# A 1,024-token two-block network on one core: where the second feed-forward's combined inputs are formed

## The chip, the cores and the metric

One core of one Trainium2 chip. The metric is the device time of one execution in microseconds (us). All data is float32; TensorE (PE) multiplies it as pairs of rounded parts (below). The kernel is written by hand in five instruction queues: PE, ACT (ScalarE), DVE (VectorE), POOL (GpSimd) and SP, which issues the DMAs. Each queue runs in its written order, and semaphores are the only link between them.

## What is computed

The whole network is a first block (pooling mixer, attention, feed-forward, gated embedding) and a second one (modulation, a token mixer, a convolutional feed-forward). The change touches the second block's feed-forward alone:

```python
h = rms_norm_2(x, pre_ffn_g[l]) * (1.0 + sc2) + sh2      # x: 1024 tokens x 1024 channels
u = causal_dwconv(h @ w_up, conv_w, conv_b)              # w_up: 1024 x 5632, 3 taps
g, val = u[..., :2816], u[..., 2816:]
y = (jax.nn.gelu(g, approximate=True) * val) @ w_down    # w_down: 2816 x 1024
x = x + g2 * rms_norm_2(y, post_ffn_g[l])
```

## The kernel before, in words

**Numbers.** Channels lie on the 128 partitions, tokens along the row: `x_mid`, `y`, `h_hi` and `h_lo` hold 8 rows (k) of 128 channels by 1024 tokens; a half is 512 tokens. A value v is carried as a rounded high part (a cast by ACT) and a low part (v minus the high part, by DVE; for weights by POOL). A product is three matmuls: high x high, low input x high weight, high input x low weight.

**Tiles.** w_up has 44 column tiles of 128: gate tile i and up tile i, for i from 0 to 21. Tiles 0 and 1 are computed plainly, in PE's order gate 0 and up 0 (both interleaved, half 0 and then half 1), gate 1, up 1 (L1475 to L1497). From tile 2 (`PLAIN`) on, the gate and the up product of a pair are made together from seven half-sized products (`product`, L979) in the order UP_LOW, SUM_2, DIFF_3, SUM_1, UP_HIGH, GATE_HIGH, DIFF_4, a Strassen-like scheme. Four of them use combinations of the input's quarters: with lo and late the first and last four rows k, 0 and 1 the halves, DIFF_3 = late0 - lo0, SUM_2 = lo1 + DIFF_3, GATE_HIGH = late1 - SUM_2, SUM_1 = lo1 - lo0. The first three lie in `back_raw`, SUM_1 in `y`; each has a high part (`back_form_high`, ACT, L2416) and a low part (`back_form_low`, DVE, L3597). SUM_1's parts go over h_hi and h_lo. The weights' combinations are DVE's `weight_low_sum` and `weight_high_sum` (L2870, L2891); `fill_pair` on ACT (L1791) casts them and on POOL (L3854) makes the low parts, in slots that come free by products.

**Banks.** A bank is freed for SUM_1 when ACT has copied the sum of UP_LOW and SUM_2 (`back_part(i, "two", 1)`, L2477), which waits for DVE's `back_sum` (L3630), which waits for ACT's copy of UP_LOW (L2471). GATE_HIGH waits for the first gate read (`back_gate_read(i, 1)`, L3636). After every second pair comes a group of the down product (`down`, L1021): eight 128-channel outputs m, each 12 matmuls of 512 columns. From m = 2 on, it waits until output m - 2 has been taken from its bank: by ACT's copy into `y` in group 0 (L2464), by DVE's addition later (`back_add`, L3644). So `y` carries other data until group 0: the squares of the norm, the rows of the combinations.

**Forming h, and the combinations.** For each half, `normed_to_ffn` on DVE (L3535) writes x_mid * gain * norm of row k into one of two rows of `tmp` (L3550); ACT adds the shift and casts to h_hi (`h_row`, L2353), and DVE writes h_lo (`low`, L3538). Because `tmp` has two rows, row k waits for its own queue's h_lo. The shift itself is a column of `mod` for each k. The combinations need full values: POOL adds h_hi and h_lo back together (`rows_sum`, L4042: four instructions of two rows each for half 0, two for half 1's first rows), DVE does so for half 1's last rows (`late_rows`, L3607). POOL then forms DIFF_3 and SUM_2 (L4049, L4055), DVE SUM_1 and GATE_HIGH (L3615, L3622), two rows an instruction (q = 0, 1). `back_raw` lies over part of `x_mid`, so the forming waits until x_mid has been parked in memory by eight DMAs (L4385).

**Tile by tile.** A tile passes ACT's first tap (`tap_first`, L2391), two taps on DVE (`tap_rest`, L3567), ACT's gelu, DVE's product, and a high (ACT, `back_hidden_high`) and low part (DVE, `back_hidden_low`) for the down product. Plain tiles read their taps from the product's banks. Between the plain products and pair 2, DVE's order is (L3650 to L3668): last rows, taps and product of tile 0, its low part, SUM_1, taps (1, 0), weight sums, GATE_HIGH, low parts of SUM_2, DIFF_3, SUM_1, taps (1, 1), product of tile 1. ACT's is L2434 to L2453. A wait in any of these queues holds everything written behind it. At the end, pair 21 is followed by down groups 9 and 10, the additions of group 9 standing behind the product of tile 21 (L3697 to L3701).

```python
            for q in range(2):
                back_form_low(SUM_1, q)
            whole_rest(1, 1, pairs.whole(("up2", 1)))
            ffn_product(1)
```

## Time and profile before

| | us |
|---|---|
| median of 3 runs | 2787.8 (2786.1 to 2792.4) |
| the profiled execution | 2787.0 |
| its span | 2785.2 |
| PE busy | 2668.6 (96%) |
| DVE busy | 1634.5 (59%) |
| ACT busy | 1111.0 (40%) |
| POOL busy | 1079.3 (39%) |
| mean granted clock of PE | 0.987 of full |

The profiled execution is one run; its span is the time from its first to its last instruction, and 1.8 us lie around it. Busy shares say how much an engine worked over the whole span, not whether the others waited for it. All stretches below are in us from the span's start. The second feed-forward begins near 2061 us and its pair 2 near 2119 us.

### The profile page before, as it was taken

The page shows a single profiled execution, that of the slowest core. Times are in us where ns is not written, and L with a number is a line of the kernel's source. Part 1 is how long each engine was busy: PE and PEld are TensorE (multiplying, and loading weights), DVE is VectorE, ACT ScalarE, POOL GpSimd, SP SyncE. Part 2 cuts the span into 40 slices and gives each one's busy share as a digit, 9 for nine tenths or more (in the row PEclk, how much of TensorE's full clock was granted, in tenths as well). Part 3 has the DMA queues.
Part 4 walks back from the last instruction along what each step waited for, and adds up shares of the span by engine and source line. Part 5 has one row for each costly group of instructions (what it writes and reads, how often), then busy time and mean ns, then how long its engine had stood idle before and what let it go on. Part 6 is the DMA issues. An engine that isn't in the chain of part 4 may idle for free.

```text
span 2785.2 us, 31774 instructions
## 1 busy us (share of the span) xinstructions
PE 2668.6 (96%) x12096; PEld 2135.2 (77%) x12096; DVE 1634.5 (59%) x1877; ACT 1111.0 (40%) x1888; POOL 1079.3 (39%) x705
## 2 busy tenths in 40 slices
PE   8999989999999999999999999999987999999997
PEld 6666768888778888888877678778756888888885
DVE  6777776652855555555663646527367465565656
ACT  6666521113533333233353433455344433343343
POOL 2444422224444444344444321123445444444445
PEclk9999999999999999999999999999999999999999
DMA  3000034433111111111212111122321111111113
GB/s 120 23 24 24 3 122 154 153 118 114 38 46 61 46 61 61 46 46 61 70 44 101 62 39 38 43 70 72 121 83 32 59 46 46 61 46 61 60 46 136
DMA packets 72055, 185.03 MB, mean 66 GB/s; under 512 B 7384, under 2 KB 20952, under 8 KB 71776
## 3 DMA queue, kind: packets, MB, share of 16 engines
q1 hardware_dynamic: 71904, 183.01, 19.9%
q8 instruction: 96, 1.57, 0.2%
q14 instruction: 55, 0.45, 0.1%
HBM read 167.71 MB, written 15.27 MB: 66 GB/s over the span
## 4 chain that ended last, share of the span: by engine, by line
PE 81%; DVE 9%; issue 3%; ACT 3%; POOL 2%; DMA 1%; SPq 0%; DVEq 0%; POOLq 0%; ACTq 0%
PE psum_mem L998 27%; PE psum_mem L704 17%; PE psum_mem L1038 16%; PE psum_mem L766 2%; PE psum_mem L1190 2%; PE psum_mem L1195 2%; PE psum_mem L1192 2%; PE psum_mem L750 2%; PE psum_mem L801 1%; PE psum_mem L856 1%; PE psum_mem L804 1%; PE psum_mem L802 1%; PE psum_mem L1267 1%; POOL w_lo L3759 1%; PE psum_mem L1232 1%
## 5 line engine op out<-in xcount | busy, mean ns | idle before, releaser
L3851 POOL TENSOR_TENSOR w_lo<-w_raw,w_hi 128x512 fp32r<-128x512 f32 x298 | 434.1, 1463 | 498.1 <-ACT w_hi L1789 497.6
L3759 POOL TENSOR_TENSOR w_lo<-w_raw,w_hi 128x1024 fp32r<-128x1024 f32 (+2 forms) x105 | 236.1, 2249 | 636.5 <-ACT w_hi L1559 591.3
L1789 ACT CAST w_hi<-w_raw 128x512 fp32r<-128x512 f32 x298 | 182.5, 620 | 297.8 <-PE psum_mem L998 115.4
L998 PE MATMUL psum_mem<-h_hi,w_hi 128*128 128x512 f32 x672 | 265.0, 394 | 15.0 <-ACT norm_row L2426 8.5
L998 PE MATMUL psum_mem<-h_hi,w_lo 128*128 128x512 f32 x672 | 264.0, 393 | 0.6 <-POOL w_lo L3851 0.6
L998 PE MATMUL psum_mem<-h_lo,w_hi 128*128 128x512 f32 x672 | 263.8, 393 | 0.0
L704 PE MATMUL psum_mem<-h_hi,w_hi 128*128 128x512 f32 x736 | 234.8, 400 | 14.0 <-ACT h_hi L1593 8.8
L704 PE MATMUL psum_mem<-h_hi,w_lo 128*128 128x512 f32 x736 | 230.0, 394 | 3.5 <-POOL w_lo L3759 3.5
L704 PE MATMUL psum_mem<-h_lo,w_hi 128*128 128x512 f32 x736 | 230.7, 395 | 2.6 <-DVE h_lo L3483 2.2
L1559 ACT CAST w_hi<-w_raw 128x1024 fp32r<-128x1024 f32 (+2 forms) x105 | 100.2, 954 | 270.9 <-PE psum_mem L704 242.5
L704 PEld LDWEIGHTS psum_mem<-h_hi,w_hi 128*128 128x128 f32 x736 | 138.7, 191 | 47.3 <-ACT h_hi L1593 8.8
L704 PEld LDWEIGHTS psum_mem<-h_hi,w_lo 128*128 128x128 f32 x736 | 139.7, 190 | 35.1 <-POOL w_lo L3759 5.6
L704 PEld LDWEIGHTS psum_mem<-h_lo,w_hi 128*128 128x128 f32 x736 | 139.7, 190 | 34.6 <-DVE h_lo L3483 3.4
L2996 DVE TENSOR_TENSOR x_block<-x_block,psum_mem 128x1024 f32<-128x1024 f32 x88 | 107.3, 1219 | 93.8 <-PE psum_mem L1038 93.7
L998 PEld LDWEIGHTS psum_mem<-h_hi,w_hi 128*128 128x128 f32 x672 | 127.6, 190 | 44.3 <-ACT norm_row L2426 9.4
L998 PEld LDWEIGHTS psum_mem<-h_hi,w_lo 128*128 128x128 f32 x672 | 127.5, 190 | 27.9 <-POOL w_lo L3851 1.3
L998 PEld LDWEIGHTS psum_mem<-h_lo,w_hi 128*128 128x128 f32 x672 | 127.5, 190 | 26.8 <-DVE h_lo L2903 0.4
L3809 POOL TENSOR_TENSOR beta<-beta,left 128x128 f32<-128x128 f32 (+2 forms) x96 | 87.6, 914 | 142.5 <-DVE left L2702 141.6
L1190 PE MATMUL psum_mem<-h_hi,w_hi 128*128 128x512 f32 x272 | 113.2, 416 | 4.6 <-POOL state L3970 3.4
L3648 DVE TENSOR_TENSOR y_mem<-y_mem,psum_mem 128x1024 f32<-128x1024 f32 x72 | 87.5, 1216 | 48.1 <-PE psum_mem L1038 47.9
L1195 PE MATMUL psum_mem<-h_hi,w_lo 128*128 128x512 f32 x272 | 107.2, 394 | 0.0
L998 PE MATMUL psum_mem<-form_hi,w_hi 128*128 128x512 f32 x264 | 103.0, 390 | 3.8 <-ACT form_hi L1809 2.1
(457 smaller groups left out, 6333.2 us busy)
## 6 DMA issues: line engine op xcount, KB each, us to landing
w_raw<-in_w_up_b SPq DMA_DIRECT2D x44, 512.0 KB, 3.3
w_raw<-in_w_in_a SPq DMA_DIRECT2D x32, 512.0 KB, 3.4
ada_raw<-in_w_ada SPq DMA_DIRECT2D x64, 256.0 KB, 3.3
w_raw<-in_w_ffn_up SPq DMA_DIRECT2D x22, 512.0 KB, 3.2
w_raw<-in_w_ffn_gate SPq DMA_DIRECT2D x22, 512.0 KB, 3.3
w_raw<-in_w_ffn_down SPq DMA_DIRECT2D x22, 512.0 KB, 3.2
w_raw<-in_w_down_b SPq DMA_DIRECT2D x22, 512.0 KB, 3.3
merged<-in_w_ada SPq DMA_DIRECT2D x32, 256.0 KB, 3.2
```

Of the source, the lines that this page charges most:

```text
L704: made = e.matmul(pairs.half(use, half), wt, x[:, half_of(half)], start=at == 0 and part == 0, stop=at == len(rhs) - 1 and part == 2, skip ...
L998: made = e.matmul(out, wt, x, start=j <= DIFF_3 and k == 0 and part == 0, stop=k == KH - 1 and part == 2, skip_group_check=True)
L1038: made = e.matmul(out[:, half, :], wt, x[:, half_of(half)], start=i == 0 and part == 0, stop=i == FFN_GROUP - 1 and part == 2, skip_group_ ...
L1190: e.matmul(bank(6 + half), high, h_hi[:, k, cols], start=k == 0, stop=False, skip_group_check=True)
L1195: made = e.matmul(bank(6 + half), low, h_hi[:, k, cols], start=False, stop=k == KD - 1, skip_group_check=True)
L1559: e.copy(w_hi[:, i, 0:width], w_raw[:, i, 0:width]).then_inc(*S.of("w_hi", c))
L1789: e.copy(w_slot(w_hi, slot, of), source).then_inc(*S.of("w_hi", key))
L2996: e.tensor_tensor(x1[:, m, :], x1[:, m, :], down_banks(g, m), ALU.add).then_inc(*S.of("x1", (g, m)))
L3648: e.tensor_tensor(y[:, m, :], y[:, m, :], down_banks(g, m), ALU.add).then_inc(*S.of("y_add", (g, m)))
L3759: e.tensor_tensor(w_lo[:, i, 0:width], w_raw[:, i, 0:width], w_hi[:, i, 0:width].bitcast(F32), ALU.subtract).then_inc(*S.of("w_lo", c))
L3809: e.tensor_tensor(kept, kept, left[i % 3][:, HALF + 1 - width:HALF + 1], ALU.mult).then_inc(*S.of("weight", i))
L3851: e.tensor_tensor(w_slot(w_lo, slot, of), source, w_slot(w_hi, slot, of).bitcast(F32), ALU.subtract).then_inc(*S.of("w_lo", key))
```

## The change

Four things, in the order of the diff:

- The normalised rows (before the shift) are kept in `y` for all k, where they were in two rows of `tmp`; h_hi and h_lo are made from there. The wait of row k on the own h_lo is gone.
- The combinations are formed on DVE from these rows, the difference of shifts (`gain[:, 0:KH]`, 128x4) or the shift being added in the same instruction: DIFF_3, SUM_2 and GATE_HIGH by four instructions of one row each, SUM_1 by two of two rows as before. POOL's six sums and four combinations and DVE's two sums of last rows are gone.
- Orders. ACT: DIFF_3's high parts ahead of gelu of tile 0; tap (1, 0) behind SUM_2's; gelu of tile 1 behind all of pair 2's first fills; tile 1's high part behind two fills of down group 0. DVE: DIFF_3 and SUM_2 ahead of tile 0's taps; SUM_1 and GATE_HIGH behind its product; low parts in the order DIFF_3, SUM_2, then taps (1, 0), then SUM_1; taps (1, 1), product and low part of tile 1 behind pair 2's first gate read.
- At the end, the first two additions of down group 9 stand between the taps of tile 21 and its product; tile 21's low part follows the third.

```diff
@@ -2354,7 +2354,7 @@
                 cols = half_of(half)
                 w.wait_ge("normed", ("ffn2", k, half))
                 w.wait_ge("full", ("out2", KD - 1, 1))
-                e.activation(h_hi[:, k, cols], tmp[:, k % 2, cols], ACT.Identity,
+                e.activation(h_hi[:, k, cols], y[:, k, cols], ACT.Identity,
                              bias=mod[:, 3 * KD + k:3 * KD + k + 1], scale=1.0).then_inc(*S.of("h_hi", ("ffn2", k, half)))
 
...
@@ -2414,7 +2414,7 @@
             def back_form_high(j, q):
-                w.wait_ge("form_g" if j in (DIFF_3, SUM_2) else "form", ("b", j, q))
+                w.wait_ge("form", ("b", j, 2 * q + 1))
...
@@ -2434,14 +2434,13 @@
             plain_tap(0, 0)
             plain_tap(0, 1)
             unit()
-            gelu(0)
             for q in range(2):
                 back_form_high(DIFF_3, q)
+            gelu(0)
             back_hidden_high(0)
-            plain_tap(1, 0)
             for q in range(2):
                 back_form_high(SUM_2, q)
-            gelu(1)
+            plain_tap(1, 0)
             fill_pair(PLAIN, UP_LOW, "b")
             fill_pair(PLAIN, SUM_2, "b")
             for q in range(2):
@@ -2449,8 +2448,9 @@
             for q in range(2):
                 back_form_high(GATE_HIGH, q)
             fill_pair(PLAIN, DIFF_3, "b")
+            fill_pair(PLAIN, SUM_1, "b")
+            gelu(1)
             plain_tap(1, 1)
-            fill_pair(PLAIN, SUM_1, "b")
             taken[0], done[0] = len(units), len(units)
 
             for kind, at in FF_ORDER[PLAIN:-2]:
@@ -2475,7 +2475,8 @@
                 if i > PLAIN:
                     w.wait_ge("gate", ("b", i - 1, 0))
                 back_part(i, "two", 1)
-                back_hidden_high(i - 1)
+                if i > PLAIN:
+                    back_hidden_high(i - 1)
                 fill_pair(i, DIFF_4, "b")
                 w.wait_ge("full", ("gu2", i, SUM_1))
                 back_part(i, "four", 0)
@@ -2486,6 +2487,8 @@
                 else:
                     fill_pair(i + 1, UP_LOW, "b")
                     fill_pair(i + 1, SUM_2, "b")
+                if i == PLAIN:
+                    back_hidden_high(1)
                 w.wait_ge("gate", ("b", i, 0))
                 tap_first(i, 0, gate_in[:, :])
                 if g is None:
@@ -3537,7 +3540,7 @@
 
                 def low(k):
                     w.wait_ge("h_hi", ("ffn2", k, half))
-                    e.scalar_tensor_tensor(out=h_lo[:, k, cols], in0=tmp[:, k % 2, cols],
+                    e.scalar_tensor_tensor(out=h_lo[:, k, cols], in0=y[:, k, cols],
                                            scalar=mod[:, 3 * KD + k:3 * KD + k + 1],
                                            in1=h_hi[:, k, cols].bitcast(F32), op0=ALU.add,
                                            op1=ALU.subtract).then_inc(*S.of("h_lo", ("ffn2", k, half)))
@@ -3545,9 +3548,7 @@
                 w.own("x_mid")
                 w.wait_ge("x_mid_g", (MID_POOL[-1], half))
                 for k in range(KD):
-                    if k >= 2:
-                        w.own("h_lo")
-                    e.scalar_tensor_tensor(out=tmp[:, k % 2, cols], in0=x_mid[:, k, cols],
+                    e.scalar_tensor_tensor(out=y[:, k, cols], in0=x_mid[:, k, cols],
                                            scalar=gain[:, 2 * KD + k:2 * KD + k + 1], in1=norm, op0=ALU.mult,
                                            op1=ALU.mult).then_inc(*S.of("normed", ("ffn2", k, half)))
                     if k > 0:
@@ -3596,36 +3597,39 @@
 
             def back_form_low(j, q):
                 w.wait_ge("form_hi", ("b", j, q))
-                if j == DIFF_3:
-                    w.wait_ge("form_g", ("b", SUM_2, q))
                 low = back_form(back_lo_mem, h_lo, j, q)
                 source = y[:, two_rows(q), half_of(0)] if j == SUM_1 else back_form(back_raw, None, j, q)
...
-            def late_rows(q):
-                rows, cols = two_rows(q, 1), half_of(1)
-                w.wait_ge("sum", ("mid", 1))
-                w.wait_ge("h_hi", ("ffn2", KD - 1, 1))
-                w.own("h_lo")
-                e.tensor_tensor(y[:, rows, cols], h_hi[:, rows, cols].bitcast(F32), h_lo[:, rows, cols].bitcast(F32),
-                                ALU.add).then_inc(*S.of("form", ("b", "late", q)))
+            def shift(k):
+                return mod[:, 3 * KD + k:3 * KD + k + 1]
+
+            def back_form_three(k):
+                w.own("shift")
+                w.own("normed")
+                e.scalar_tensor_tensor(out=back_raw[:, BACK_FORMS.index(DIFF_3), k, :], in0=y[:, KH + k, half_of(0)],
+                                       scalar=gain[:, k:k + 1], in1=y[:, k, half_of(0)], op0=ALU.add,
+                                       op1=ALU.subtract).then_inc(*S.of("form", ("b", DIFF_3, k)))
+
+            def back_form_two(k):
+                w.own("form")
+                e.scalar_tensor_tensor(out=back_raw[:, BACK_FORMS.index(SUM_2), k, :], in0=y[:, k, half_of(1)],
+                                       scalar=shift(k), in1=back_raw[:, BACK_FORMS.index(DIFF_3), k, :], op0=ALU.add,
+                                       op1=ALU.add).then_inc(*S.of("form", ("b", SUM_2, k)))
+
+            def back_form_four(k):
+                w.own("form")
+                e.scalar_tensor_tensor(out=back_raw[:, BACK_FORMS.index(GATE_HIGH), k, :], in0=y[:, KH + k, half_of(1)],
+                                       scalar=shift(KH + k), in1=back_raw[:, BACK_FORMS.index(SUM_2), k, :],
+                                       op0=ALU.add, op1=ALU.subtract).then_inc(*S.of("form", ("b", GATE_HIGH, k)))
 
             def back_form_one(q):
                 rows = two_rows(q)
-                w.wait_ge("form_g", ("b", "rows", 1, q))
-                w.wait_ge("form_g", ("b", DIFF_3, q))
+                w.own("form")
                 e.tensor_tensor(y[:, rows, half_of(0)], y[:, rows, half_of(1)], y[:, rows, half_of(0)],
-                                ALU.subtract).then_inc(*S.of("form", ("b", SUM_1, q)))
-
-            def back_form_four(q):
-                w.own("form")
-                w.wait_ge("form_g", ("b", SUM_2, q))
-                e.tensor_tensor(back_form(back_raw, None, GATE_HIGH, q),
-                                y[:, two_rows(q, 1), half_of(1)],
-                                back_form(back_raw, None, SUM_2, q),
-                                ALU.subtract).then_inc(*S.of("form", ("b", GATE_HIGH, q)))
+                                ALU.subtract).then_inc(*S.of("form", ("b", SUM_1, 2 * q + 1)))
 
             def back_sum(i):
                 w.wait_ge("part", ("b", i, "low"))
@@ -3647,25 +3651,29 @@
-            for q in range(2):
-                late_rows(q)
+            for k in range(KD):
+                w.wait_ge(f"parked{k}", "mid")
+            e.tensor_tensor(gain[:, 0:KH], mod[:, 3 * KD + KH:4 * KD], mod[:, 3 * KD:3 * KD + KH],
+                            ALU.subtract).then_inc(*S.of("shift", 0))
+            for k in range(KH):
+                back_form_three(k)
+            for k in range(KH):
+                back_form_two(k)
             whole_rest(0, 0, pairs.whole(("gate2", 0)))
             whole_rest(0, 1, pairs.whole(("up2", 0)))
             ffn_product(0)
-            back_hidden_low(0)
             for q in range(2):
                 back_form_one(q)
-            whole_rest(1, 0, pairs.whole(("gate2", 1)))
+            for k in range(KH):
+                back_form_four(k)
+            back_hidden_low(0)
             weight_low_sum(PLAIN, "b")
-            for q in range(2):
-                back_form_four(q)
-            for j in (SUM_2, DIFF_3):
+            for j in (DIFF_3, SUM_2):
                 for q in range(2):
                     back_form_low(j, q)
+            whole_rest(1, 0, pairs.whole(("gate2", 1)))
             for q in range(2):
                 back_form_low(SUM_1, q)
-            whole_rest(1, 1, pairs.whole(("up2", 1)))
-            ffn_product(1)
 
             for kind, at in FF_ORDER[PLAIN:-2]:
                 if kind == "down":
@@ -3677,14 +3685,19 @@
                         if m == 3:
                             weight_low_sum(2 * at + 3, "b")
                     continue
-                i, g = at, down_behind(at)
+                i, g = at, N_GROUPS - 2 if at == KF - 1 else down_behind(at)
                 back_sum(i)
                 weight_high_sum(i, "b")
                 if i == PLAIN:
                     for q in range(2):
                         back_form_low(GATE_HIGH, q)
-                back_hidden_low(i - 1)
-                back_gate_read(i, 1)
+                    back_gate_read(i, 1)
+                    whole_rest(1, 1, pairs.whole(("up2", 1)))
+                    ffn_product(1)
+                    back_hidden_low(1)
+                else:
+                    back_hidden_low(i - 1)
+                    back_gate_read(i, 1)
                 if g is None and i < KF - 1:
                     weight_low_sum(i + 1, "b")
                 back_gate_read(i, 0)
@@ -3695,9 +3708,9 @@
                         back_add(g, added_so_far)
                         added_so_far += 1
                 ffn_product(i)
-            for m in range(KD):
+            for m in range(2, KD):
                 back_add(N_GROUPS - 2, m)
-                if m == 1:
+                if m == 2:
                     back_hidden_low(KF - 1)
 
 
@@ -4039,39 +4052,9 @@
             ahead(2)
             normed_sum(1)
 
...
-            for late in range(2):
-                for q in range(2):
-                    rows_sum(late, 0, q)
             taken[0] += 2
             ahead(1)
-            for q in range(2):
-                rows_sum(0, 1, q)
-            for k in range(KD):
-                w.wait_ge(f"parked{k}", "mid")
-            w.wait_ge("h_lo", ("ffn2", KD - 1, 1))
             unit()
-            for q in range(2):
-                back_form_three(q)
-                back_form_two(q)
             for j in (UP_LOW, SUM_2, DIFF_3, SUM_1):
                 fill_pair(PLAIN, j, "b")
             taken[0], done[0] = len(units), len(units)
```

## Rows read from the trace of the kernel before

**Rows 1.** The page, part 1: busy time, share of the span, instructions.
```profile
PE 2668.6 (96%) x12096; PEld 2135.2 (77%) x12096; DVE 1634.5 (59%) x1877; ACT 1111.0 (40%) x1888; POOL 1079.3 (39%) x705
```

**Rows 2.** Waits, 2094 to 2160: engine and line, awaited, total us, times, longest.
```profile
ACT back_form_hi L2423 <- POOL back_raw L4051: 11.3, 2, 7.4
...
ACT norm_row L2426 <- DVE psum_mem L3634: 10.6, 1, 10.6
...
PE psum_mem L998 <- ACT norm_row L2426: 8.1, 1, 8.1
...
PE psum_mem L998 <- ACT w_hi L1789: 4.2, 1, 4.2
```

**Rows 3.** Busy time by stretch: engines, then granted clock, DMA share, GB/s.
```profile
core 0: us, PE busy (x) PEld busy (x) DVE busy (x) ACT busy (x) POOL busy (x), PEclk, DMA share, GB/s
2135.00:2146.00 11.00, 2.41 (x7) 1.69 (x8) 10.86 (x10) 1.62 (x3) 3.81 (x2) 0.77 0.16 49
```

**Rows 4.** Timeline of POOL, 2058 to 2110: start, us, line, out<-in, idle before.
```profile
2065.89 2.38 POOL L4046 TENSOR_TENSOR y_mem<-h_hi,h_lo 128x1024 f32<-128x1024 f32 x1 [3.65 <-DVE h_lo L3540]
...
2095.87 2.38 POOL L3759 TENSOR_TENSOR w_lo<-w_raw,w_hi 128x1024 fp32r<-128x1024 f32 x1 [15.01 <-ACT w_hi L1559]
...
2102.93 3.38 POOL L3759 TENSOR_TENSOR w_lo<-w_raw,w_hi 128x1024 fp32r<-128x1024 f32 x1
```

**Rows 5.** Timeline of DVE, 2058 to 2094.
```profile
2066.45 2.38 DVE L3540 SCALAR_TENSOR_TENSOR h_lo<-tmp_mem,mod,h_hi 128x512 fp32r<-128x512 f32 x1
...
2079.03 2.39 DVE L3106 SCALAR_TENSOR_TENSOR psum_mem<-tmp_mem,next_row 128x512 f32<-128x512 f32 x1
...
2081.46 1.41 DVE L3550 SCALAR_TENSOR_TENSOR tmp_mem<-x_mid,gain,psum_mem 128x512 f32<-128x512 f32 x2
...
2085.23 0.75 DVE L3550 SCALAR_TENSOR_TENSOR tmp_mem<-x_mid,gain,psum_mem 128x512 f32<-128x512 f32 x1
2085.89 0.75 DVE L3540 SCALAR_TENSOR_TENSOR h_lo<-tmp_mem,mod,h_hi 128x512 fp32r<-128x512 f32 x1
2086.67 0.75 DVE L3550 SCALAR_TENSOR_TENSOR tmp_mem<-x_mid,gain,psum_mem 128x512 f32<-128x512 f32 x1
...
2091.67 1.63 DVE L3540 SCALAR_TENSOR_TENSOR h_lo<-tmp_mem,mod,h_hi 128x512 fp32r<-128x512 f32 x2
```

**Rows 6.** Timeline of PE, 2058 to 2162.
```profile
2068.88 0.50 PE L750 MATMUL psum_mem<-h_lo,w_hi 128*128 128x512 f32 x1 [1.42 <-DVE h_lo L3540]
...
2083.01 0.80 PE L750 MATMUL psum_mem<-h_hi,w_hi 128*128 128x512 f32 x1 [2.44 <-ACT h_hi L2357]
...
2098.30 0.74 PE L704 MATMUL psum_mem<-h_hi,w_lo 128*128 128x512 f32 x2 [1.20 <-POOL w_lo L3759]
...
2119.10 0.39 PE L750 MATMUL psum_mem<-h_hi,w_lo 128*128 128x512 f32 x1
...
2145.02 0.79 PE L998 MATMUL psum_mem<-h_hi,w_hi 128*128 128x512 f32 x1 [8.07 <-ACT norm_row L2426]
...
2157.38 0.62 PE L1038 MATMUL psum_mem<-hid_hi_b,w_hi 128*128 128x512 f32 x2
```

**Rows 7.** ACT's groups, 2094 to 2165: count, busy us, mean ns, idle before.
```profile
L2423 ACT CAST back_form_hi<-back_raw 128x1024 fp32r<-128x1024 f32 x6 | 6.2, 1048 | 12.3 <-POOL back_raw L4051 11.3 <-DVE back_raw L3625 1.0
L1789 ACT CAST w_hi<-w_raw 128x512 fp32r<-128x512 f32 x10 | 6.1, 616 | 4.7 <-PE psum_mem L998 4.7
```

**Rows 8.** Chain that ended last, 2090 to 2180: start, us, what.
```profile
2157.54 21.76 PE psum_mem L1038 x96
```

**Rows 9.** Parking DMAs, L4385: ns min/median/max, first and last start.
```profile
L4385 SPq DMA_DIRECT2D x_park<-x_mid x8: 319/326/1032, 2053.5 to 2062.3; - x8
```

**Rows 10.** DVE's groups, 2094 to 2165.
```profile
L3574 DVE SCALAR_TENSOR_TENSOR tmp_mem<-psum_mem,vecs,tmp_mem 128x1023 f32<-128x1023 f32 x5 | 6.4, 1278 | 1.4 <-ACT tmp_mem L2400 1.2
...
L3625 DVE TENSOR_TENSOR back_raw<-y_mem,back_raw 128x1024 f32<-128x1024 f32 x2 | 4.5, 2246 | 0.0
...
L3619 DVE TENSOR_TENSOR y_mem<-y_mem 128x1024 f32<-128x1024 f32 x2 | 2.3, 1212 | 0.0
```

**Rows 11.** Timeline of ACT: the first copy of down 0 to y.
```profile
2161.49 1.01 ACT L2464 COPY y_mem<-psum_mem 128x1024 f32<-128x1024 f32 x1
```

**Rows 12.** Timeline of PE at group 9 of the down product.
```profile
2723.11 0.73 PE L1038 MATMUL psum_mem<-hid_hi_b,w_hi 128*128 128x512 f32 x2 [1.79 <-DVE y_mem L3648]
```

16 lines of the change are left out of this document (removed).

## The prediction, made before the changed kernel was run

> **What bounds the kernel now.** The page's first part says TensorE (PE): 96% busy [rows 1], so time can only go where PE stands still or runs slow. The waits from 2094 to 2160 us show the one place where it stands long [rows 2]: 8.1 us for `norm_row` (L2426, the copy of UP_LOW's part that frees SUM_2's bank for SUM_1) and 4.2 us for the first weights of pair 2. ACT's copy stood behind DVE's b_sum (L3634). The table of stretches shows what it costs: PE is busy 2.4 of the 11 us from 2135 on, and the granted clock falls to a mean of 0.77, so for a time to its lower level of 1.2 GHz [rows 3]. What makes DVE late is read in its queue: it can't finish tile 1 and the low parts of the forms before ACT has DIFF_3 from POOL, and ACT waited 11.3 us for POOL's combinations [rows 2].
>
> A second place is earlier. While POOL adds h_hi and h_lo back together (L4046, 2.38 us each [rows 4]), a DVE instruction with two SBUF inputs that meets one stands until it is over: L3540 takes 2.38 us for 0.75, L3106 2.39 us [rows 5]. PE waits 1.4 us for three such h_lo and 2.4 us for the start of half 1 [rows 6].
>
> **Part 1, POOL's sums gone (half 0).** Four L4046 stood in the way. Without them, and without the wait on the own h_lo (pair start to start 1.32 us by L3540 to L3550 0.66, for 1.44 now [rows 5]), DVE's low(0) stays at 2063.6, since ACT's first h_row waits for a square. ACT's three 128x512 instructions of the second inverse (near the 0.62 us of a w_hi each [rows 7], 2.0 with their waits) now fall between h_row 3 and 4 and hold DVE 1.1 us. low(7) comes at 2073.4, the inverse's two steps take 1.45 us instead of 3.1, and normed(0) of half 1 starts at 2075.5, now 2081.5 [rows 5]: **-5.9 us**. PE, needing 1.36 us a row for both weights (six matmuls at 0.227, from 96 in 21.76 us [rows 8]), ends half 0 at 2075.8 and waits 1.3 us instead of 2.4.
>
> **Half 1 and the plain products.** From h_hi at 2077.1 PE is the slower (1.36 us a row against DVE's 1.32). The seven matmuls that start slowly at 2083.0 (the first 0.80 us long [rows 6]) cost 1.3 us, and after the shorter pause I count them fast. PE ends half 1 7.2 us earlier, still waits 1.2 us for gate 1's w_lo [rows 6], and ends up 1 at 2112.1, now 2119.4 [rows 6].
> POOL's w_lo of gate 1 becomes ready at 2088.6 in the middle of DVE's new train. The two let each other in by turns: POOL's w_lo at 2102.93 took 3.38 us, an instruction of DVE more than the 2.38 of the other [rows 4]. Between 0 and 1.0 us for PE; I take 0.2, since one 0.75 us DVE instruction is half over then.
>
> **Part 2, the sums on DVE.** low(7) ends at 2086.7 (now 2093.3 by [rows 5]). Gone are two L3612 (2.4 us). The eight waits on parked rows cost nothing: the last DMA was issued at 2062.3, 24 us before [rows 9]. The 128x4 difference of shifts has no row of its size; it lies between nothing and 0.75 (a 128x512 one), I take 0.2, its fixed part. Then 4 DIFF_3 at 0.66, 4 SUM_2 at 0.78 (each waits for its predecessor; start to start by [rows 5]), later 4 GATE_HIGH at 0.78: 8.9 us for twelve. For these, the Trainium skill, "VectorE: DVE Perf Modes", The TRN2 errata, charges every instruction its fixed 151 cycles and advises few large ones, against this change; its formula gives 0.69 us each, 8.3 in all, and the result would be 0.6 us earlier.
> The last DIFF_3 meets the w_lo of gate 1 and the first SUM_2 that of up 1 (2.4 us each [rows 4]): SUM_2 is formed at 2097.0 with 4.2 us of blocking. The taps of tile 0 (4 at 1.28 and a little, PSUM source [rows 10]) run to 2102.3, the product to 2103.6, form_one (1.21 each [rows 10]) to 2106.0, GATE_HIGH to 2109.1, hidden_low(0) to 2111.6 with 1.3 of blocking, the weight sums to 2113.8, the four low parts of DIFF_3 and SUM_2 (1.21 each, clean) with 1.3 of blocking to 2119.9, the taps (1,0) to 2122.5, low SUM_1 to 2124.9. The blocking in this list is the unknown term: 7 us taken, 3.5 if half of the meetings miss, 11 if every w_lo is met as L3625 was (2.25 for 1.21 [rows 10]).
>
> **ACT.** DIFF_3's high parts go ahead of gelu(0) (2 casts of 1.05 [rows 7]), hidden in its wait for the taps. hidden_high(0) ends 2104.8, high SUM_2 2106.6, tap (1,0) 2107.8, w_hi UP_LOW 2108.4, long before PE asks at 2112.1, so the **4.2 us wait goes**. w_hi SUM_2 follows the weight sums at 2114.5, four high casts to 2118.4, w_hi DIFF_3 and SUM_1 to 2119.6. gelu(1) is queued ahead of the part of UP_LOW and waits for DVE's taps (1,0): 2122.6 to 2123.6, tap (1,1) to 2124.8, part low 2125.3.
>
> **PE in pair 2.** UP_LOW 2112.1 to 2114.9. SUM_2 then waits for its low part, 3.6 us (new), to 2121.4; DIFF_3 to 2124.1. b_sum 2125.4 to 2126.1; ACT has two w_hi (0.62 [rows 7]) queued ahead of part two, ready 2126.95. **SUM_1 starts at 2127.0 instead of 2145.0 [rows 6]: -18.0 us**, of which 7.2 are from before. The wait is 2.9 instead of 8.1 us. A slow clock between 2118 and 2124 falls into that wait.
>
> **What is moved behind it.** Tile 1's taps (1,1), product and low part now stand between the two gate reads. weight_high_sum and the two low GATE_HIGH end at 2132.8, gate read 2133.5: PE's GATE_HIGH waits 1.0 us. Down 0 can begin at 2139.0. Taps (1,1) 2136.1, product 2137.4, high part 2138.5 (behind the w_hi of slot 1, which needs GATE_HIGH full at 2136.3), low part 2139.8, in time for its second weight (2140.8). But gate read 0, taps (2,0), gelu(2) and two w_hi follow, and only then ACT's first y copy (1.0 us, now at 2161.5 [rows 11], ready 0.3 us before PE asks for it, 24 matmuls or 5.4 us into down 0 [rows 6, 8]). It now comes at 2147.4, and PE asks at 2144.5: **a new wait of 2.9 us**. Third matmul group of down 0: 2147.4 instead of 2162.8: **-15.4**. Behind it two groups lie between each copy and its use, and the DMAs of pair 3, issued as w_lo slots come free (2148.6, 17 us earlier), keep ahead; no stall is left there now and I expect none.
>
> **The end.** PE waits 1.8 us for y_add of group 9 [rows 12], which stands behind the last product. Put between the taps it ends at 2720.5, before PE asks at 2721.3; the second ends 2723.0, before 2724.0. Tile 21's product comes 2.5 us later, but down 10 needs it only 12 us on. **-1.8**.
>
> **Sum.** -15.4 - 1.8 = -17.2 against the profiled execution of 2787.0 us (span 2785.2): 2769.8, taken as 2770. The runs' median is 2787.8; its 0.8 us is under what I can place. About 0.2% (5.6 us) is what a measurement can tell from no change.
>
> **Rivals.**
> A, DVE and POOL meet less: half of the 7 us of blocking goes, then SUM_1 starts at about 2123.5 and the y copy is 3.5 us earlier: 2766, and to 2763 if none is left. For: POOL has only two long and some ten short operations there. Against: every long one has met DVE so far. Chance 0.15. The Trainium skill, "SBUF — State Buffer", Who interferes with whom, has the lock held for a whole instruction by whoever starts first, so that the order of issue decides; both outcomes fit it.
> B, the long L3540 have another cause than POOL (cause and time coincide three times, no run shows it). Then half 1 starts as now, 5.9 later than forecast; DVE's list moves with it and is critical all the way: 2776. Chance 0.12.
> C, the list on DVE is as bad as the old one: the blocking costs 11 us or more, and low clock after the waits (0.2 us a matmul) is paid in down 0 too: about 8 more, 2778 to 2785, within 0.2% at its upper end. Chance 0.1, of it 0.06 as no change.
> D, slower: DVE becomes the bound from 2087 to b_sum. That list has 26 instructions with two SBUF inputs; if nearly each were held like L3625 (+1.04 us), 27 us instead of the 7 counted, SUM_1 would start at 2147, the moved tile 1 would add its 2.6 us, and the result is 2790 to 2795. It decides from some 17 us above my count. Against: POOL has no 26 operations to meet. Chance 0.04.
> That the change does nothing is no case: the sums leave POOL's queue by the diff. The forecast has the other 0.59, 2766 to 2775 by itself. Faster by over 0.2%: 0.90 (forecast, A, B, 0.04 of C); no change 0.06; slower 0.04. Range 2762 to 2779: A, B and the best of C, some 0.87.
>
> **What would show it.** No POOL operation but the w_lo in 2062 to 2105, L3540 at 0.75 throughout, normed(0) of half 1 at 2075.5; PE's wait before pair 2 gone; a wait of about 3.6 us at SUM_2 for the low part and 2.9 at SUM_1; one of about 3 us at the third group of down 0, for the y copy; none at 2721. Wrong if L3540 stays long, or if PE's SUM_1 starts past 2133.

## The result, and the profile after

The changed kernel takes 2773.0 us (median of 4 runs, 2771.7 to 2773.4) against 2786.9 for the kernel before in the same session: a ratio of 0.9946, 95% interval 0.9929 to 0.9963, so 13.9 us faster. Forecast were 2770 in a range of 2762 to 2779. The profiled execution took 2773.1 us, its span is 2771.3.

The page's first part, which answers to [rows 1]:

```profile
PE 2666.6 (96%) x12096; PEld 2135.8 (77%) x12096; DVE 1629.5 (59%) x1886; ACT 1110.6 (40%) x1888; POOL 1051.2 (38%) x695
```

PE did the same 12096 matmuls in almost the same busy time; what went is time in which it stood. The waits of PE from 2058 to 2170 us, for [rows 2] (engine and line, awaited, total us, times, longest):

```profile
PE psum_mem L1038 <- ACT y_mem L2464: 3.5, 1, 3.5
PE psum_mem L998 <- DVE back_form_lo L3603: 2.5, 1, 2.5
PE psum_mem L759 <- ACT y_mem L2350: 1.6, 1, 1.6
PE psum_mem L704 <- POOL w_lo L3772: 1.2, 1, 1.2
PE psum_mem L750 <- ACT h_hi L2357: 0.9, 1, 0.9
PE psum_mem L998 <- ACT norm_row L2426: 0.7, 1, 0.7
PE psum_mem L750 <- DVE h_lo L3543: 0.6, 2, 0.3
PE psum_mem L998 <- DVE gate_conv_in L3645: 0.4, 1, 0.4
```

The 8.1 and 4.2 us before SUM_1 and pair 2 are now 0.7 and nothing, the three h_lo of 4.2 in all are two of 0.6, the start of half 1 costs 0.9 for 2.4. In their place stand the two new waits of the forecast: 2.5 us for SUM_2's low part and 3.5 for ACT's first y copy.

**One origin for all runs.** Stretches that the change does not touch vary from profile to profile, so every moment below is given from the start of DVE's first normalised row of half 0 (L3550 before, L3551 after). That row starts at 2061.15 us before and at 2064.24 after, though no earlier code differs. "End" is the span less that moment.

| us from that row | half 1's first row | pair 2 starts | SUM_1 starts | down 0 starts | its third output | pair 3 starts | end |
|---|---|---|---|---|---|---|---|
| before | 20.3 | 62.6 | 83.9 | 96.2 | 101.7 | 118.0 | 724.0 |
| after | 14.1 | 50.7 | 64.2 | 75.9 | 85.1 | 104.1 | 707.1 |
| e1 POOL's sums back | 19.9 | 58.0 | 69.9 | 82.5 | 90.8 | 108.7 | 712.3 |
| e2 end as before | 14.1 | 51.3 | 64.0 | 75.8 | 84.8 | 103.8 | 709.0 |
| e3 copies first | 14.1 | 51.3 | 64.0 | 75.7 | 81.1 | 103.9 | 706.9 |
| e4 gelu 1 first | 14.1 | 59.5 | 69.6 | 80.5 | 88.8 | 106.8 | 709.8 |
| e5 SUM_2's low parts first | 14.1 | 51.3 | 64.0 | 76.4 | 84.9 | 104.1 | 707.0 |
| e6 ACT's unit later | 14.1 | 50.7 | 64.1 | 75.9 | 85.1 | 104.1 | 707.1 |
| e7 e5 and b_sum early | 14.1 | 50.7 | 63.1 | 75.8 | 84.0 | 102.0 | 704.9 |
| e10 slots 2, 3 early | 14.1 | 51.3 | 63.9 | 75.7 | 84.1 | 102.0 | 705.0 |
| e9 e3 and e10 | 14.1 | 51.3 | 64.0 | 75.7 | 81.1 | 97.8 | 700.8 |
| e8 e5, e6, e7, e9 | 14.1 | 50.7 | 63.1 | 74.5 | 80.0 | 96.7 | 699.6 |
| e11 e6, held | 14.1 | 51.3 | 61.9 | 74.5 | 82.8 | 100.8 | 703.8 |
| e12 e8, held | 14.1 | 50.7 | 61.1 | 72.6 | 78.1 | 94.7 | 697.7 |

Counted so, the change is worth 724.02 - 707.06 = 17.0 us (17.2 forecast). Between the two profiled executions 13.9 us are left of it, as the changed one reaches the origin 3.1 us later. The last column can also be held against the medians: median less "end" is 2062.9 for the kernel before and 2061.4 to 2065.3 for the seven other kernels with more than one run, but 2066.0 for the changed one. So the medians' 13.9 is probably smaller than 17.0 for the same reason, but only one execution of each kernel was profiled. By medians e1 is 2.9 us above the changed kernel, and e2, e3 and e4 are 2.6, 3.3 and 0.2 below it; that is not the order of the last column. The readings of the experiments rest on the table, with one profile for each kernel. What speaks for it is that equal code agrees in it: half 1's first row is at 14.1 wherever POOL's sums are gone, and from pair 3 to the end eleven of the fourteen kernels take 602.93 to 602.95 us (not the kernel before, e1 and e2).

DVE's timeline, for [rows 5] (start, us, line, out<-in, idle before):

```profile
2069.28 0.75 DVE L3543 SCALAR_TENSOR_TENSOR h_lo<-y_mem,mod,h_hi 128x512 fp32r<-128x512 f32 x1
...
2077.59 0.70 DVE L3109 SCALAR_TENSOR_TENSOR psum_mem<-tmp_mem,next_row 128x512 f32<-128x512 f32 x1
2078.32 1.41 DVE L3551 SCALAR_TENSOR_TENSOR y_mem<-x_mid,gain,psum_mem 128x512 f32<-128x512 f32 x2
...
2089.34 0.16 DVE L3656 TENSOR_TENSOR gain<-mod 128x4 f32<-128x4 f32 x1
2089.53 4.91 DVE L3612 SCALAR_TENSOR_TENSOR back_raw<-y_mem,gain 128x512 f32<-128x512 f32 x4
2094.47 5.14 DVE L3618 SCALAR_TENSOR_TENSOR back_raw<-y_mem,mod,back_raw 128x512 f32<-128x512 f32 x4
2099.53 5.30 DVE L3575 SCALAR_TENSOR_TENSOR tmp_mem<-psum_mem,vecs,tmp_mem 128x1023 f32<-128x1023 f32 x4
...
2115.92 5.72 DVE L3603 TENSOR_TENSOR back_form_lo<-back_raw,back_form_hi 128x1024 fp32r<-128x1024 f32 x4
...
2126.84 0.70 DVE L3638 TENSOR_TENSOR psum_mem<-psum_mem,norm_row 128x512 f32<-128x512 f32 x1 [0.43 <-ACT norm_row L2426]
```

No h_lo in the stretch is long any more, L3109 takes 0.70 us for 2.39, and between the last row of half 0 and the start of half 1 nothing stands. The 128x4 difference cost 0.16 us (0.2 taken). Then the four DIFF_3 take 4.91 us and the four SUM_2 5.14, where 2.7 and 3.1 would do, because of POOL:

```profile
2091.52 2.37 POOL L3772 TENSOR_TENSOR w_lo<-w_raw,w_hi 128x1024 fp32r<-128x1024 f32 x1 [26.19 <-ACT w_hi L1559]
2094.65 2.84 POOL L3772 TENSOR_TENSOR w_lo<-w_raw,w_hi 128x1024 fp32r<-128x1024 f32 x1 [0.76 <-ACT w_hi L1559]
```

These two w_lo (POOL's timeline, for [rows 4]; nothing of POOL stands in the 26.2 us before them) hold DVE 2.2 and 2.0 us. PE's timeline, for [rows 6]:

```profile
2120.56 0.71 PE L998 MATMUL psum_mem<-back_form_lo,w_hi 128*128 128x512 f32 x1 [2.53 <-DVE back_form_lo L3603]
...
2145.20 0.61 PE L1038 MATMUL psum_mem<-hid_hi_b,w_lo 128*128 128x512 f32 x2
2149.34 1.22 PE L1038 MATMUL psum_mem<-hid_hi_b,w_hi 128*128 128x512 f32 x2 [3.52 <-ACT y_mem L2464]
2150.35 1.06 PE L1038 MATMUL psum_mem<-hid_lo_b,w_hi 128*128 128x512 f32 x2
...
2155.18 0.63 PE L1038 MATMUL psum_mem<-hid_lo_b,w_hi 128*128 128x512 f32 x2
```

Two matmuls of down 0 take 0.61 us before the wait and 1.06 behind it, for some 5 us. The table of stretches says why (columns as in [rows 3]):

```profile
2146.00:2149.40 3.40, 0.06 (x1) 0.07 (x1) 3.15 (x4) 3.11 (x5) 1.40 (x2) 0.79 0.00 0
2149.40:2153.00 3.60, 3.60 (x9) 2.86 (x10) 0.95 (x1) 1.31 (x2) 3.32 (x2) 0.50 0.14 22
2153.00:2157.00 4.00, 4.00 (x15) 3.23 (x14) 2.08 (x3) 1.02 (x1) 0.00 (x0) 0.77 0.28 112
2157.00:2161.00 4.00, 4.00 (x19) 3.30 (x18) 0.00 (x0) 2.12 (x3) 1.29 (x1) 1.00 0.02 4
```

The granted clock is 0.50 of full behind the wait, its lower level of 1.2 GHz, and full again from 2157 us on at the latest. ACT's timeline shows that the high parts of DIFF_3 and SUM_2 no longer wait (11.3 us before, [rows 2]), and what the copy stood behind, for [rows 11]:

```profile
2094.47 2.00 ACT L2423 CAST back_form_hi<-back_raw 128x1024 fp32r<-128x1024 f32 x2
...
2107.15 2.00 ACT L2423 CAST back_form_hi<-back_raw 128x1024 fp32r<-128x1024 f32 x2
...
2146.29 1.06 ACT L2406 ACTIVATE tmp_mem<-tmp_mem 128x1024 f32<-128x1024 f32 x1 [1.58 <-DVE tmp_mem L3575]
2147.25 1.12 ACT L1789 CAST w_hi<-w_raw 128x512 fp32r<-128x512 f32 x2
2148.28 1.92 ACT L2464 COPY y_mem<-psum_mem 128x1024 f32<-128x1024 f32 x2
```

### The profile page after: what moved, and what is told of

Read it like the earlier page. It is cut to its first block, busy times and chain, and to the rows that moved or that the text cites. A ratio compares the mean times of both kernels' runs of the same rounds, so it can differ in the third digit from the quotient of the medians.

```text
span 2771.3 us, 31769 instructions
## 1 busy us (share of the span) xinstructions
PE 2666.6 (96%) x12096; PEld 2135.8 (77%) x12096; DVE 1629.5 (59%) x1886; ACT 1110.6 (40%) x1888; POOL 1051.2 (38%) x695
## 3 DMA queue, kind: packets, MB, share of 16 engines
q1 hardware_dynamic: 71904, 183.01, 19.9%
## 4 chain that ended last, share of the span: by engine, by line
PE 82%; DVE 9%; ACT 3%; issue 2%; POOL 2%; DMA 1%; SPq 0%; DVEq 0%; POOLq 0%; ACTq 0%
PE psum_mem L998 27%; PE psum_mem L704 18%; PE psum_mem L1038 16%; PE psum_mem L766 2%; PE psum_mem L1190 2%; PE psum_mem L1195 2%; PE psum_mem L1192 2%; PE psum_mem L750 1%; PE psum_mem L801 1%; PE psum_mem L856 1%; PE psum_mem L804 1%; PE psum_mem L802 1%; PE psum_mem L1267 1%; PE psum_mem L1232 1%; PE psum_mem L1534 1%
## 5 line engine op out<-in xcount | busy, mean ns | idle before, releaser
L998 PE MATMUL psum_mem<-h_lo,w_hi 128*128 128x512 f32 x672 | 261.7, 389 | 1.3 <-DVE h_lo L2906 1.3
L704 PE MATMUL psum_mem<-h_lo,w_hi 128*128 128x512 f32 x736 | 230.5, 395 | 3.0 <-DVE h_lo L3486 2.7
L1192 PE MATMUL psum_mem<-h_lo,w_hi 128*128 128x512 f32 x272 | 107.1, 394 | 0.0
```

Source lines behind the costliest of these rows:

```text
L704: made = e.matmul(pairs.half(use, half), wt, x[:, half_of(half)], start=at == 0 and part == 0, stop=at == len(rhs) - 1 and part == 2, skip ...
L998: made = e.matmul(out, wt, x, start=j <= DIFF_3 and k == 0 and part == 0, stop=k == KH - 1 and part == 2, skip_group_check=True)
L1192: e.matmul(bank(6 + half), high, h_lo[:, k, cols], start=False, stop=False, skip_group_check=True)
```

## The experiments

All are edits of the changed kernel. The theory is that of the forecast.

### e1: POOL's sums of half 0 back (5 runs)

```diff
+            for late in range(2):
+                for q in range(2):
...
+                    e.tensor_tensor(gate_in[:, :].rearrange("p (a b) -> p a b", a=2),
+                                    h_hi[:, rows, half_of(0)].bitcast(F32), h_lo[:, rows, half_of(0)].bitcast(F32),
+                                    ALU.add).then_inc(*S.of("unused", (late, q)))
             taken[0] += 2
             ahead(1)
```

> The changed kernel, plus the four sums h_hi + h_lo of half 0 back on POOL at their old place, written to memory that nobody reads. Theory 1 (a DVE instruction with two inputs in SBUF stands still while POOL adds): L3543 of 2.3 to 2.4 us beside three of the sums again, L3109 too, row 0 of half 1 formed 5 to 6 us later after row 0 of half 0 than in the changed kernel (14.1 us there, 19.5 to 20.3 here), and, if DVE's list is what PE then waits for all the way to down group 0, the whole kernel 5 to 6 us slower, about 2778.5. Rival B (the long L3540 had another cause): every L3543 at 0.75, 14.1 us, the time unchanged at 2773. Second rival (the early gain is absorbed by the later waits): the half starts 5 to 6 us later, but the total moves by under 3.

DVE's timeline, then POOL's:

```profile
2069.45 2.45 DVE L3543 SCALAR_TENSOR_TENSOR h_lo<-y_mem,mod,h_hi 128x512 fp32r<-128x512 f32 x1
...
2081.86 2.39 DVE L3109 SCALAR_TENSOR_TENSOR psum_mem<-tmp_mem,next_row 128x512 f32<-128x512 f32 x1
```

```profile
2068.95 2.40 POOL L4061 TENSOR_TENSOR gate_conv_in<-h_hi,h_lo 128x1024 f32<-128x1024 f32 x1 [3.46 <-DVE h_lo L3543]
...
2081.30 2.39 POOL L4061 TENSOR_TENSOR gate_conv_in<-h_hi,h_lo 128x1024 f32<-128x1024 f32 x1 [1.29 <-DVE h_lo L3543]
```

Nobody waits for these sums, and yet the long DVE instructions are back, each beside one. Half 1's first row comes 5.8 us later, the end 5.3 us; of these 0.7 arise 207 us behind the start of pair 3, where PE waits 0.5 us for ACT's copy to `norm_row` (0.4 in the kernel before, nothing in the changed one; why is open). Rival B falls: POOL's sums themselves were the cause. The last 0.4 us to the kernel before, 20.3 against 19.9, may be the wait on the own h_lo, which was not tried alone.

### e2: the end as before (4 runs)

```diff
-                i, g = at, N_GROUPS - 2 if at == KF - 1 else down_behind(at)
+                i, g = at, down_behind(at)
...
-            for m in range(2, KD):
+            for m in range(KD):
                 back_add(N_GROUPS - 2, m)
-                if m == 2:
+                if m == 1:
```

> The changed kernel with the end of DVE's queue as before: no addition of group 9 between the taps of tile 21. Theory: PE again waits 1.8 us at the third output of group 9, and group 10 starts 1.8 us later after pair 21; time +1.8, 2774.8. Rival: the end's gain is nil, because another wait takes its place; then no difference in the trace between pair 21 and group 10.

Its waits of PE from 2690 us on hold one row; the changed kernel has none there:

```profile
PE psum_mem L1038 <- DVE y_mem L3652: 1.9, 1, 1.9
```

From the origin the end is 1.9 us later, as forecast (1.8); from pair 3 on, behind which the two kernels differ only there, it is 605.2 us against 602.9, so 2.2: the wait and some slow matmuls behind it. The median of its runs is 2770.4, though, below that of the changed kernel: a difference of this size is not to be had from medians here.

### e3: ACT's first two y copies ahead of gelu and fills (4 runs)

```diff
                 tap_first(i, 1, up_banks(i))
+                if i == PLAIN:
+                    w.wait_ge("form_lo", ("b", GATE_HIGH, 1))
+                    w.wait_ge("form_lo", ("b", SUM_1, 1))
+                    y_copy(0)
                 gelu(i)
+                if i == PLAIN:
+                    y_copy(1)
```

(`y_copy(m)` is the wait for output m and the copy of L2464; these two copies are left out at the old place.)

> The changed kernel with ACT's first two copies of down group 0 moved: the first ahead of gelu of tile 2, the second right behind it, both ahead of the two weight fills. Theory: the 3.5 us wait of PE at the third output goes, and with it the slow clock that followed (35 matmuls in 10.8 us, 2.9 us more than at full clock); gelu and DVE's product of tile 2 come 0.3 to 0.9 us later, unnoticed. Time -3.5 to -6.5, 2766.5 to 2769.5. Rival 1: the wait is only handed on, to w_lo of slots 2 and 3 or to tile 2's product, total within 1 us. Rival 2: slow clock comes anyway, at another place: -3.5 only.

The third output came 4.0 us earlier and without a wait, and yet the end came only 0.2 us earlier: rival 1. Four timelines, PE, ACT, DVE and POOL, read from the last to the first:

```profile
2155.95 1.02 PE L1038 MATMUL psum_mem<-hid_hi_b,w_hi 128*128 128x512 f32 x2 [4.39 <-ACT y_mem L2436]
```

```profile
2154.37 0.62 ACT L1789 CAST w_hi<-back_w_sums 128x512 fp32r<-128x512 f32 x1 [7.20 <-DVE back_w_sums L2899]
2154.89 1.92 ACT L2436 COPY y_mem<-psum_mem 128x1024 f32<-128x1024 f32 x2
```

```profile
2152.12 0.69 DVE L2889 SCALAR_TENSOR_TENSOR back_w_sums<-w_raw 128x512 f32<-128x512 f32 x1 [6.16 <-DMA w_raw<-in_w_up_b]
```

```profile
2143.59 4.77 POOL L3873 TENSOR_TENSOR w_lo<-w_raw,w_hi 128x512 fp32r<-128x512 f32 x3 [8.43 <-ACT w_hi L1789]
```

The seventh output waits 4.4 us for ACT's copy of the fifth, the first of the two in its row. Both copies stand behind a cast of pair 3's weight sums; DVE forms those from rows whose DMA is issued only once POOL has made the w_lo of down 0's slots 2 and 3, and ACT casts these slots behind gelu of tile 2. The copy and the slots are two limits of nearly one date, and the prediction's "no stall is left there now" held only while the first was there.

### e10 and e9: slots 2 and 3 early, alone (1 run) and with e3's copies (5 runs)

```diff
                 if i == PLAIN:
                     back_hidden_high(1)
+                    fill_down(g, 2, "b")
+                    fill_down(g, 3, "b")
                 w.wait_ge("gate", ("b", i, 0))
```

(and the later place left out for `i == PLAIN`)

> The changed kernel with ACT's fills of slots 2 and 3 of down group 0 ahead of tile 2's taps instead of behind its gelu. The copy experiment showed a second limit behind the first: the second row of pair 3's weights is loaded only when POOL has read slots 2 and 3, and fill SUM_2 of pair 3, which waits for it, stands in ACT's queue ahead of the copies of outputs 4 and 5. Theory: here the first copy comes 1.1 us earlier (84.0), and the load lands 5 to 6 us earlier; the wait at the third output is 2.4 instead of 3.5, no other wait in group 0. Rival: tile 2's taps are delayed by the fills and the first copy gains nothing.

> Both moves together: the first two copies ahead of and behind gelu of tile 2, slots 2 and 3 filled ahead of tile 2's taps. Theory (the wait at the third output has two limits in series, the copy and, 10 us later, the load of pair 3 behind slots 2 and 3): no wait of PE in group 0, no slow clock after it; pair 3 begins 98.0 to 98.5 from the start of the stretch, where the changed kernel has 104.1 and the copy move alone 103.9; the whole 5 to 6 us faster than the changed kernel, 2767 to 2768 by the median. Rival: a third limit (gelu and product of tile 2, weight sums of pair 3) takes the gain back, pair 3 at 103 or later.

Alone it gives 2.1 us: the copy has two casts less before it, the wait is 2.8 us and the third output 1.0 us earlier; the other 1.1 us is a shorter slow stretch behind the wait (7 slow matmuls, 13 in the changed kernel). Together with the copies PE has no wait in group 0, pair 3 starts 6.3 us earlier, and the end too. The median of e9 is 2766.0, ratio to the kernel before 0.9919 (0.9905 to 0.9933). This pair also prices the clock: from the third output to pair 3 it is 16.7 us in e9, 16.3 in the kernel before, and 19.0 in the changed one. The slow stretch behind the wait costs 2.7 us against the kernel before (2.4 against e9, where two matmuls are slow too) on top of the 3.5.

### e4: ACT's gelu of tile 1 ahead of the fills (4 runs)

```diff
             plain_tap(1, 0)
+            gelu(1)
             fill_pair(PLAIN, UP_LOW, "b")
...
             fill_pair(PLAIN, SUM_1, "b")
-            gelu(1)
```

> The changed kernel with ACT's gelu of tile 1 back ahead of the weight fills of pair 2, where it was before. Theory (the place of this gelu is what removed PE's 4.2 us wait before pair 2): it waits for DVE's taps (1, 0), which now end near 2124 us, so the first weights of pair 2 come at 2125 instead of 2110 and PE stands 9 to 11 us before pair 2; b_sum is then bound by PE and not by DVE; time +5 to +9, 2778 to 2782. Rival (PE in pair 2 is bound by b_sum behind DVE's list anyway, so that the place of the gelu is worth little): under +2.

```profile
PE psum_mem L998 <- ACT w_hi L1789: 8.6, 1, 8.6
PE psum_mem L1038 <- ACT y_mem L2464: 2.7, 1, 2.7
```

PE waits 8.6 us before pair 2 (its waits from 2094 us on), twice what it did before the change, and still the end is only 2.7 us later, the third output 3.7. The 5 to 9 us that were expected did not come, and neither did the rival's "under +2". PE got most of it back: pair 2 starts 8.8 us later, but the waits at SUM_2, SUM_1 and GATE_HIGH (2.5, 0.7 and 0.4) are gone, the copy's is 0.8 shorter and the slow stretch behind it 1.0, so pair 3 is only 2.7 us late. These waits are for things that follow from DVE's list, which the gelu hardly holds: its low parts of SUM_1 start 1.0 us later from the origin. The gelu's place is worth 2.7 us in the changed kernel, not the length of the wait that it removes.

### e5, e6 and e7: three orders round DVE's list (1 run each)

```diff
-            for j in (DIFF_3, SUM_2):
+            for j in (SUM_2, DIFF_3):
                 for q in range(2):
                     back_form_low(j, q)
```

> The changed kernel with the low parts in the order SUM_2, DIFF_3, as before the change. Times below are from the start of DVE's first normalised row of half 0 in each trace, so that nothing ahead of the changed stretch counts. Theory (DVE's list as a whole bounds pair 2 and what follows): PE's 2.5 us wait at SUM_2 goes, the one at SUM_1 grows by as much; SUM_1 at 64.2 as in the changed kernel, third output of down group 0 at 85.1, both within 0.5. Rival (the 2.5 us wait is on the path): SUM_1 and the rest 2 us earlier.

```diff
-            unit()
             for q in range(2):
                 back_form_high(DIFF_3, q)
+            unit()
             gelu(0)
```

> The changed kernel with ACT's cast of up 1's weights behind the high parts of DIFF_3, so that POOL's low part of them runs beside DVE's taps (one input in PSUM) and not beside the four SUM_2. Theory 1: the four SUM_2 take 3.1 us instead of 5.1, the taps keep their 1.3 us each, and all of DVE's list, SUM_1 (62.2 for 64.2) and the third output of group 0 (83.1 for 85.1) come 2 us earlier. Rival: POOL's operation meets the product or another two-input instruction instead and the gain is under 0.7 us; or PE stands for up 1's weights.

```diff
             whole_rest(1, 0, pairs.whole(("gate2", 1)))
+            back_sum(PLAIN)
             for q in range(2):
                 back_form_low(SUM_1, q)
```

(on top of e5, with ACT's copy of UP_LOW and the fill of UP_HIGH moved ahead of gelu of tile 1)

> The changed kernel with SUM_2's low parts first, ACT's copy of UP_LOW's part and the UP_HIGH fill ahead of gelu of tile 1, and DVE's b_sum ahead of SUM_1's low parts. Theory: PE starts SUM_1 about 2 us earlier (62 from the start of the stretch) and DVE's weight_high_sum no longer waits 1.2 us for w_lo; but the third output of group 0 hangs on tile 1 and tile 2 at the end of DVE's list, so it comes at most 1.5 us earlier (83.6 to 85.1) and the wait there grows by the rest. Rival: the whole of the 2 us arrives at the third output.

e5 takes away SUM_2's wait; instead DIFF_3 waits 1.0 us for POOL's w_lo and SUM_1 3.0 us. SUM_1 starts where it did and so does pair 3: sum nothing. e6 gives nothing either: the second w_lo starts later in DVE's list but still meets its SUM_2. e7 brings b_sum earlier: SUM_1 1.0 us (2 were expected), the third output 1.1, the end 2.2, the same as e10, because again the slow stretch behind it shrank.

### e8: all of them (4 runs)

> All moves of the other experiments together on the changed kernel: low parts of SUM_2 first, part of UP_LOW and b_sum early, up 1's weights cast later, the first copies and slots 2 and 3 early. Theory: DVE's list is 2 us shorter where the SUM_2 meet POOL no longer and 1.2 us at weight_high_sum, group 0 begins 3 us earlier than in the changed kernel and runs without a wait; pair 3 at 95 to 96 from the start of the stretch (104.1 in the changed kernel), the whole 8 to 9 us faster than it, 2764 to 2765. Rival: PE, whose own work from the first plain product is the floor, or ACT's queue leaves under 6.

Pair 3 starts 7.5 us earlier than in the changed kernel and the end as much, less than the 8 to 9 expected: e6's move again does not spare the four SUM_2, which take 5.13 us. Median 2763.5, ratio 0.9911 (0.9897 to 0.9925).

### e11 and e12: the second w_lo held until DVE reads the banks (1 and 4 runs)

In e6 the second w_lo came some 3 us too early, so one more wait puts POOL's w_lo beside the taps, which take one input from PSUM:

```diff
             for q in range(2):
                 back_form_high(DIFF_3, q)
+            w.wait_ge("form", ("b", SUM_2, 3))
             unit()
```

> The changed kernel with ACT's cast of up 1's weights held until the fourth SUM_2 is formed, so that POOL's low part of them surely runs beside DVE's taps of tile 0, whose source is in PSUM (the earlier run moved it too little: POOL still met the SUM_2). Theory (POOL and DVE exclude each other only where DVE reads two inputs from SBUF, and DVE's list bounds PE until down group 0): the four SUM_2 take 3.1 us instead of 5.1, the four taps stay at 5.3, SUM_1 starts at 62.1 for 64.2 from the start of the stretch, third output at 83.0 for 85.1, pair 3 at 102.0. Rival: taps are blocked as well, 7.3 us, and nothing moves.

> The version with all moves, with the same hold on up 1's weights. Theory: DVE's list 2 us shorter there too; pair 3 at 94.7 for 96.7 from the start of the stretch, 2761.5 by the median. Rival: in this version DVE's list is no longer what bounds pair 2, since ACT's parts and fills stand between: under 1 us.

DVE's timeline of e11, then POOL's, then DVE's of e12:

```profile
2088.17 2.74 DVE L3613 SCALAR_TENSOR_TENSOR back_raw<-y_mem,gain 128x512 f32<-128x512 f32 x4
2090.95 5.10 DVE L3619 SCALAR_TENSOR_TENSOR back_raw<-y_mem,mod,back_raw 128x512 f32<-128x512 f32 x4
2095.96 5.30 DVE L3576 SCALAR_TENSOR_TENSOR tmp_mem<-psum_mem,vecs,tmp_mem 128x1023 f32<-128x1023 f32 x4
```

```profile
2090.20 2.93 POOL L3773 TENSOR_TENSOR w_lo<-w_raw,w_hi 128x1024 fp32r<-128x1024 f32 x1 [26.23 <-ACT w_hi L1559]
2097.21 2.42 POOL L3773 TENSOR_TENSOR w_lo<-w_raw,w_hi 128x1024 fp32r<-128x1024 f32 x1 [4.07 <-ACT w_hi L1559]
```

```profile
2084.22 4.91 DVE L3628 SCALAR_TENSOR_TENSOR back_raw<-y_mem,gain 128x512 f32<-128x512 f32 x4
2089.16 3.11 DVE L3634 SCALAR_TENSOR_TENSOR back_raw<-y_mem,mod,back_raw 128x512 f32<-128x512 f32 x4
2092.19 5.30 DVE L3591 SCALAR_TENSOR_TENSOR tmp_mem<-psum_mem,vecs,tmp_mem 128x1023 f32<-128x1023 f32 x4
```

The w_lo at 2097.21 lies wholly inside the taps, which take the same 5.30 us as without it, and it takes 2.42 us itself. The first w_lo still meets one instruction: 4 DIFF_3 are 2.74 clean and 4.91 met, 4 SUM_2 3.11 clean and 5.10 met. One meeting costs 2.0 to 2.2 us. SUM_1 starts 2.2 us earlier in e11 and the end comes 3.3 us earlier, as the slow stretch behind the y copy is 1.0 us shorter. From the origin e12 gains 1.9 us on e8: median 2759.7 (2758.4 to 2762.6), ratio to the kernel before 0.990 (0.9883 to 0.9916), the fastest of all. PE's waits in it from 2094 us on are one row:

```profile
PE psum_mem L998 <- ACT norm_row L2426: 2.0, 1, 2.0
```

## Why the prediction was right, step by step

- **Part 1.** Half 1's first row 14.1 us after the origin, 14.35 forecast (-6.2 us, -5.9 forecast). PE's wait for it 0.9 (1.3). e1 undoes 5.8 of the 6.2.
- **The plain products.** Their last matmul ended 50.9 us after the origin, 51.0 forecast. Gate 1's wait for its w_lo is 1.2 us as before.
- **Twelve forms in 8.9 us.** Clean, four DIFF_3 take 2.74 us: three starts at 0.66 and a last of 0.75. Four SUM_2 take 3.11: at 0.78. Both as taken. The formula of the Trainium skill, "VectorE: DVE Perf Modes", The TRN2 errata, stated there for an fp32 tensor_tensor, makes 0.69 us of 512 elements. The forms are scalar_tensor_tensor; the rows stand on both sides of it, 0.66 without and 0.78 us with a wait for the predecessor.
- **Blocking of 7 us in DVE's list.** Measured against clean durations: DIFF_3 2.2, SUM_2 2.0, GATE_HIGH 1.0 (3.12 clean in e4), the four low parts 1.1: 6.3 us. Rivals A and D fall with that, and of C the blocking. The Trainium skill, "SBUF — State Buffer", Who interferes with whom, has a DVE instruction with two SBUF inputs contend with a GpSimd one that reads SBUF, and one with a single SBUF input not at all. e11 and e12 agree: 2.0 to 2.2 us for the train that meets a w_lo, nothing for the taps.
- **Part 2 as a whole** was not undone by any run. That the combinations on DVE remove the long wait is read from the rows: ACT's 11.3 us for POOL's combinations are nothing now, and SUM_1 starts 19.7 us earlier, of which e1 gives back 5.8.
- **Pair 2.** The 4.2 us wait went. SUM_2 waits 2.5 us (3.6 forecast), SUM_1 0.7 (2.9), GATE_HIGH 0.4 (1.0). SUM_1 starts 19.7 us earlier from the origin, 18.0 forecast. "A slow clock between 2118 and 2124 falls into that wait" was right about why the next wait is short: PE ran slow behind SUM_2's wait (granted clock 0.83 between 2120 and 2130 us) and so asked for SUM_1 late.
- **Down 0.** Third output 85.1 us after the origin, 86.3 forecast: -16.6 for -15.4. Its wait was 3.5 us (2.9).
- **Behind it: the term that was missing.** Behind the third output the sum counts nothing. From there to pair 3 the changed kernel takes 19.0 us, the kernel before 16.3: +2.7. Thirteen matmuls behind the new wait start 0.43 us apart where 0.23 is the pitch at full clock, 2.7 us in all. Only rival C had a price for it ("low clock after the waits (0.2 us a matmul) is paid in down 0 too"). e9 shows that the wait brings it: without the wait two matmuls are slow.
- **The end.** -1.8 forecast, 2.2 by e2, counted from pair 3.
- **Sum.** 16.6 - 2.7 + 2.2 = 16.1. Of the other 0.9 us, 0.7 are the wait 207 us behind the start of pair 3, which the kernel before and e1 have and the changed one has not; the sum had no term for it. In all 17.0 against 17.2. That this agrees so well is in part luck: +1.2, +0.4 and the unforeseen 0.9 nearly cancel the -2.7.

What the sum could not hold is the time ahead of the change. One stretch of unchanged code, before and after, from the tables of stretches of the two kernels:

```profile
1530.00:1560.00 30.00, 25.12 (x94) 16.73 (x93) 26.14 (x36) 20.67 (x28) 5.05 (x2) 1.00 0.20 70
```

```profile
1530.00:1560.00 30.00, 25.64 (x87) 17.21 (x85) 24.53 (x33) 19.46 (x27) 5.05 (x2) 0.89 0.20 70
```

PE gets a clock of 1.00 there before and 0.89 after. Held against the kernel before, instruction by instruction, the changed one is 0.4 us ahead at 1535 us, 1.7 behind from 1550 on, 2.4 by 1880 and 3.1 by 1970. A slow stretch does not always cost something: between 740 and 760 us the kernel before has the lower clock (0.83, 1.00 after), and the distance between the two moves by less than 0.1 us. Over the fourteen profiles the origin lies between 2058.9 and 2064.4 us with the same code ahead of it. Why the slow stretches fall at other places was not tried; it stays open. The later origin makes 3.1 of the 3.3 us between the forecast of the profiled execution, 2769.8, and its 2773.1.

## What to carry to other kernels

When a wait goes, look for every stream that has nearly the same date behind it: here the copy hid the slots, and each alone gave 0.2 or 2.1 us while both gave 6.3. A POOL instruction that nobody waits for can still hold a DVE one with two SBUF inputs; move it beside some that read one input from PSUM. Price a new wait of PE with the slow clock behind it, and measure a local change from a landmark just ahead of it: the runs of one kernel spread over 1.7 to 7.2 us here, more than most parts of the change are worth.
